# Row sums by TensorE in the expert part of a decoder kernel, and ScalarE's gelu of the dots moved within its beat

## The reference

```python
q = (xt @ wq).reshape(t, PEER_HEADS, 2, PEER_KEY_DIM)
sc = jnp.einsum('thcd,hcnd->thcn', q, keys)
# top 16 of each half, top 16 of their pair sums: 8 heads x 16 = 128 experts per token
gate = jax.nn.softmax(top, axis=-1)
act = jax.nn.gelu(jnp.einsum('td,tkd->tk', xb, u[ib]))      # u: 16384 x 1024
y = jnp.einsum('tk,tkd->td', gb * act, v[ib])               # v: 16384 x 1024
h = h + y
```

## Time and profile before

| | |
|---|---|
| median of 3 runs | 3909.01 us (3907.59 to 3911.07) |
| the profiled execution | 3902.45 us |
| its span | 3900.3 us |
| busy: PE, DVE, ACT, POOL | 3177.5, 2572.0, 813.4, 922.5 us |
| mean granted clock of TensorE | 0.886 of full |
| moved by DMA | 943.26 MB, mean 242 GB/s |

### The profile page before, as it was taken

How to read it: one execution, slowest core, us unless ns; L and a number is a source line. 1 busy time by engine, 2 the same in 40 slices (tenths; PEclk the granted TensorE clock), 3 DMA queues, 4 the chain that set the end, 5 groups by cost and what they waited for, 6 DMA issues and landing times. The chain is left out here.

```text
span 3900.3 us, 38895 instructions
## 1 busy us (share of the span) xinstructions
PE 3177.5 (81%) x12836; PEld 2259.9 (58%) x12836; DVE 2572.0 (66%) x5206; ACT 813.4 (21%) x1764; POOL 922.5 (24%) x888
## 2 busy tenths in 40 slices
PE   6947877876699999999578478777766999999995
PEld 5725566765466666565266256666755665665652
DVE  3574554899876666666746634548998766666666
ACT  2331323236300000000033313231463000000000
POOL 0011201237422222222200122022373222222221
PEclk9969878986799999999889788788867999999997
DMA  3100112269999999999731001121799999999997
GB/s 102 54 0 1 48 37 78 67 224 287 317 408 417 416 417 417 417 417 405 307 97 38 1 1 48 44 81 65 244 290 330 413 416 417 416 417 417 413 402 289
DMA packets 235338, 943.26 MB, mean 242 GB/s; under 512 B 19584, under 2 KB 85632, under 8 KB 164864
## 3 DMA queue, kind: packets, MB, share of 16 engines
q0 software_dynamic: 73728, 536.90, 34.8%
q1 hardware_dynamic: 95360, 370.31, 24.9%
q10 hardware_dynamic: 66048, 33.56, 2.9%
HBM read 904.52 MB, written 35.65 MB: 241 GB/s over the span
## 5 line engine op out<-in xcount | busy, mean ns | idle before, releaser
L1873 PE MATMUL bank<-peer_x_late,xT 128*128 128x256 f32 x4096 | 953.7, 388 | 128.9 <-DMA xT<-in_peer_ut 82.6
L1873 PEld LDWEIGHTS bank<-peer_x_late,xT 128*128 128x128 f32 x4096 | 790.5, 195 | 350.4 <-DMA xT<-in_peer_ut 124.6
L1980 DVE CUSTOM_DVE_ANT_0 peer_slots<-peer_slots,wide 128x1024 f32<-128x1024 f32 x512 | 626.7, 1224 | 539.0 <-DMA peer_slots<-in_peer_uv,peer_rows 537.7
L1823 POOL DMA_INDIRECT peer_slots<-in_peer_uv,peer_rows x512 | 515.0, 1006 | 1547.3 <-DVE h L1992 1433.7
L1884 PE MATMUL bank<-ring,peer_acts_u 128*128 128x512 f32 x1344 | 614.7, 602 | 59.6 <-issue 38.9
L1992 DVE SCALAR_TENSOR_TENSOR h<-peer_slots,peer_coef,h 128x1024 f32<-128x1024 f32 x512 | 657.0, 1283 | 9.3
L1884 PEld LDWEIGHTS bank<-ring,peer_acts_u 128*128 128x128 f32 x1344 | 255.1, 192 | 339.7 <-issue 304.9
L1914 ACT ACTIVATE peer_coef<-peer_dots 128x2 f32<-128x2 f32 x256 | 51.7, 202 | 1373.0 <-DVE peer_dots L1980 1373.0
L1884 PE MATMUL bank<-ring,wide 128*128 128x512 f32 x704 | 324.0, 605 | 12.3 <-DVE wide L2000 12.0
L1862 PE MATMUL bank<-peer_hot 128*128 128x128 f32 x1024 | 224.1, 389 | 96.6 <-POOL peer_hot L1832 56.3
L1862 PEld LDWEIGHTS bank<-peer_hot 128*128 128x128 f32 x1024 | 197.1, 286 | 124.1 <-ACT peer_hot L1927 82.5
(11 more groups left out here) (455 smaller groups left out, 4036.3 us busy)
## 6 DMA issues: line engine op xcount, KB each, us to landing
xT<-in_peer_ut SPq DMA_DIRECT2D x256, 512.0 KB, 21.4
ring<-in_peer_uv SPq DMA_DIRECT2D x256, 512.0 KB, 21.4
gates<-peer_staging ACTq DMA_DIRECT2D x32, 1024.0 KB, 7.1
peer_staging<-gates SPq DMA_DIRECT2D x32, 1024.0 KB, 24.4
ring<-in_w_in SPq DMA_DIRECT2D x48, 512.0 KB, 3.6
ring<-in_peer_wq SPq DMA_DIRECT2D x32, 512.0 KB, 3.6
nsa_w<-in_cmp_w SPq DMA_DIRECT2D x2, 4096.0 KB, 12.1
ring<-in_w_out SPq DMA_DIRECT2D x16, 512.0 KB, 4.5
```

The source lines that it names most:

```text
L1823: nc.gpsimd.indirect_dma_start(out=p.slots[:, n % ROW_SLOTS, :], out_offset=None, in_=A["peer_uv"], in_offset=bass.IndirectOffsetOnAxis(ap ...
L1873: last = nc.tensor.matmul(k.bank[bank_of[j]][:, 0:DENSE], u_raw[:, j % U_RING, b * P:(b + 1) * P], p.x_late[:, b, :], start=b == 0, stop=b ...
L1980: nc.vector.tensor_tensor_reduce(out=u, in0=u, in1=k.wide[:, t, :], scale=1.0, scalar=0.0, op0=ALU.mult, op1=ALU.add, accum_out=p.dots[:, ...
```

## The change

Steps 0 to 47 (`EARLY`, those until four beats before the gates are done; all are of chunk 0) are summed in another way. ScalarE takes the gelu of each dot alone (`gelu_early`). Two steps later VectorE multiplies it by its gate (`coef_early`) and GpSimd makes a diagonal matrix of the 128 coefficients (`diagonal`, a 128 x 128 operation, ring of four). Three steps later TensorE multiplies the v rows by the diagonal, two matmuls of 512 columns, and adds them up in banks 5 and 6 over all early steps (`add_row` on TensorE). In beat 80 VectorE adds the two banks to `h` (`take_early`); the first V tile, which uses the same banks, waits for that.

`steps_until` is changed: 8 steps by beat 24, then three in four beats until beat 78. GpSimd no longer does the fourth gating of a quad, ScalarE does all four. ScalarE's gelu of dots stands last in its beat. `RUN_AHEAD` is 18 for 20, and the buffers of activated U tiles 20 for 22.

```diff
@@ -1509,9 +1509,9 @@
 LAG = 4
 BATCH = 2
 TILES = P
-ACTS = 22
-OWN_ACTS = 14
-RUN_AHEAD = 20
+ACTS = 20
+OWN_ACTS = 12
+RUN_AHEAD = 18
 GELU_LAG = 2
 U_RING = 4
 V_RING = 4
@@ -1537,15 +1537,21 @@
     beat = max(beat, 0)
     chosen = CHOOSE_AT[3] + PIECES
     if beat <= chosen:
-        return beat // 4
-    first = chosen // 4
+        return beat // 3
+    first = chosen // 3
     if beat <= TILES_AT - 4:
-        return first + (beat - chosen) // 2
-    first += (TILES_AT - 4 - chosen) // 2
+        return first + (beat - chosen) * 3 // 4
+    first += (TILES_AT - 4 - chosen) * 3 // 4
     if beat <= TILES_AT:
         return first + beat - (TILES_AT - 4)
     first += 4
     return first + (min(beat, BEATS) - TILES_AT) * (STEPS - first) // TILES
+
+
+LAST_EARLY = TILES_AT - 5
+EARLY = steps_until(LAST_EARLY + 1)
+DIAGONALS = 4
+COEF_LAG, SUM_LAG = 2, 3
 
 
 def u_until(beat):
@@ -1756,8 +1762,8 @@
 
 
 
-    with stage(nc, "dve_done", "shifted", "exps", "indexed", "chosen", "turned", "kept", "hot1", "hot2", "hot1_act", "hot1_pool", "spread", "copied",
-               "stored0", "stored1", "u_done", "gelus_u", "gated", "v_done", "dots", "gelus", "coefs", "summed", "y_added",
+    with stage(nc, "dve_done", "shifted", "exps", "indexed", "chosen", "turned", "kept", "hot1", "hot2", "hot1_act", "spread", "copied",
+               "stored0", "stored1", "u_done", "gelus_u", "gated", "v_done", "dots", "gelus", "early_gelus", "early_coefs", "diagonals", "coefs", "summed", "early_in", "y_added",
                "g_in0", "g_in1", *[f"u_in{n}" for n in range(U_RING)], *[f"v_in{n}" for n in range(V_RING)]) as (block, s):
         row_in = k.row_in
         u_in = [s[f"u_in{n}"] for n in range(U_RING)]
@@ -1824,20 +1830,23 @@
                                              in_offset=bass.IndirectOffsetOnAxis(ap=p.rows[:, t, pick:pick + 1], axis=0),
                                              ).then_inc(row_in[n % ROW_SLOTS], 16)
 
-            def last_gate(q):
-                if q % (QUADS // 2) == 0:
-                    pool.wait_ge(s["kept"], q // (QUADS // 2) + 1)
-                pool.wait_ge(s["hot1"], q + 1)
-                hot = p.hot1[:, 4 * (q % 2) + 3, :]
-                nc.gpsimd.tensor_scalar(hot, hot, p.picks[:, 2, 4 * q + 3:4 * q + 4], None, ALU.mult).then_inc(s["hot1_pool"], 1)
+            def diagonal(m):
+                pool.wait_ge(s["early_coefs"], m + 1)
+                if m >= DIAGONALS:
+                    pool.wait_ge(s["summed"], m - DIAGONALS + 1)
+                nc.gpsimd.tensor_scalar(p.diagonal[:, m % DIAGONALS, :], k.ident[:, :], p.coef[:, 0, m:m + 1], None,
+                                        ALU.mult).then_inc(s["diagonals"], 1)
             for n in range(ROW_SLOTS):
                 gather(n)
             for beat in range(BEATS):
-                if 0 <= beat - QUADS_AT < QUADS:
-                    last_gate(beat - QUADS_AT)
                 for n in now(steps_until, beat):
+                    if COEF_LAG <= n < EARLY:
+                        diagonal(n - COEF_LAG)
                     if n >= LAG and n - LAG + ROW_SLOTS < STEPS:
                         gather(n - LAG + ROW_SLOTS)
+                if beat == LAST_EARLY:
+                    for m in range(EARLY - COEF_LAG, EARLY):
+                        diagonal(m)
             for n in range(ROW_SLOTS):
                 pool.wait_ge(row_in[n], 16 * len(range(n, STEPS, ROW_SLOTS)))
 
@@ -1853,7 +1862,6 @@
 
             def spread_quad(q):
                 pe.wait_ge(s["hot1_act"], q + 1)
-                pe.wait_ge(s["hot1_pool"], q + 1)
                 pe.wait_ge(s["hot2"], q + 1)
                 if q >= 2:
                     pe.wait_ge(s["copied"], q - 1)
@@ -1874,11 +1882,20 @@
                                             start=b == 0, stop=b == DB - 1)
                 last.then_inc(s["u_done"], 1)
 
+            def add_row(m):
+                pe.wait_ge(s["diagonals"], m + 1)
+                for half in range(2):
+                    last = nc.tensor.matmul(k.bank[5 + half][:, :], p.diagonal[:, m % DIAGONALS, :],
+                                            p.slots[:, m % ROW_SLOTS, DM + half * 512:DM + (half + 1) * 512],
+                                            start=m == 0, stop=m == EARLY - 1)
+                last.then_inc(s["summed"], 1)
+
             def with_v(j):
                 pe.wait_ge(v_in[j % V_RING], 16 * (j // V_RING + 1))
                 pe.wait_ge(s["gated"], j + 1)
                 if j == 0:
                     pe.wait_ge(s["kept"], 2)
+                    pe.wait_ge(s["early_in"], 2)
                 for t in range(2):
                     for half in range(2):
                         last = nc.tensor.matmul(k.bank[4 + 2 * t + half][:, :], act_of(j)[:, t * P:(t + 1) * P],
@@ -1890,6 +1907,12 @@
                         turn(t)
                 if 0 <= beat - QUADS_AT < QUADS:
                     spread_quad(beat - QUADS_AT)
+                for n in now(steps_until, beat):
+                    if SUM_LAG <= n < EARLY:
+                        add_row(n - SUM_LAG)
+                if beat == LAST_EARLY:
+                    for m in range(EARLY - SUM_LAG, EARLY):
+                        add_row(m)
                 for j in now(u_until, beat):
                     with_u(j)
                 if beat >= TILES_AT:
@@ -1913,6 +1936,10 @@
                 act.wait_ge(s["dots"], (g + 1) * BATCH)
                 nc.scalar.activation(p.coef[:, t, at:at + BATCH], p.dots[:, t, at:at + BATCH], ACT.Gelu_apprx_tanh).then_inc(s["gelus"], 1)
 
+            def gelu_early(n):
+                act.wait_ge(s["dots"], n + 1)
+                nc.scalar.activation(p.coef[:, 0, n:n + 1], p.dots[:, 0, n:n + 1], ACT.Gelu_apprx_tanh).then_inc(s["early_gelus"], 1)
+
             def gelu_u(j):
                 act.wait_ge(s["u_done"], j + 1)
                 if j >= ACTS:
@@ -1922,7 +1949,7 @@
             def gates(q):
 
                 act.wait_ge(s["hot1"], q + 1)
-                for n in range(3):
+                for n in range(4):
                     hot = p.hot1[:, 4 * (q % 2) + n, :]
                     last = nc.scalar.activation(hot, hot, ACT.Copy, scale=p.picks[:, 2, 4 * q + n:4 * q + n + 1])
                 last.then_inc(s["hot1_act"], 1)
@@ -1948,15 +1975,17 @@
                         keep(t)
                 if beat == EXPS_AT[1]:
                     exps(1)
-                for n in now(steps_until, beat):
-                    if n % BATCH == BATCH - 1:
-                        gelu_step(n // BATCH)
                 if 0 <= beat - QUADS_AT < QUADS:
                     gates(beat - QUADS_AT)
                 if 0 <= beat - 1 - QUADS_AT < QUADS:
                     copy_quad(beat - 1 - QUADS_AT)
                 for j in now(u_until, beat - GELU_LAG):
                     gelu_u(j)
+                for n in now(steps_until, beat):
+                    if n < EARLY:
+                        gelu_early(n)
+                    elif n % BATCH == BATCH - 1:
+                        gelu_step(n // BATCH)
 
         @block.vector
         def _(dve):
@@ -1984,13 +2013,24 @@
                 t, pick = m // PICKS, m % PICKS
                 if m % BATCH == 0:
                     c = slice(pick, pick + BATCH)
-                    dve.wait_ge(s["gelus"], m // BATCH + 1)
+                    dve.wait_ge(s["gelus"], (m - EARLY) // BATCH + 1)
                     nc.vector.tensor_tensor(p.coef[:, t, c], p.coef[:, t, c], p.gate[:, t, c], ALU.mult).then_inc(s["coefs"], 1)
-                    dve.wait_ge(s["coefs"], m // BATCH + 1)
-                if m:
-                    dve.wait_ge(s["summed"], m)
+                    dve.wait_ge(s["coefs"], (m - EARLY) // BATCH + 1)
+                dve.wait_ge(s["summed"], m)
                 nc.vector.scalar_tensor_tensor(out=k.h[:, t, :], in0=p.slots[:, m % ROW_SLOTS, DM:2 * DM], scalar=p.coef[:, t, pick:pick + 1],
                                                in1=k.h[:, t, :], op0=ALU.mult, op1=ALU.add).then_inc(s["summed"], 1)
+
+            def coef_early(m):
+                dve.wait_ge(s["early_gelus"], m + 1)
+                nc.vector.tensor_tensor(p.coef[:, 0, m:m + 1], p.coef[:, 0, m:m + 1], p.gate[:, 0, m:m + 1],
+                                        ALU.mult).then_inc(s["early_coefs"], 1)
+
+            def take_early():
+                dve.wait_ge(s["summed"], EARLY)
+                for half in range(2):
+                    o = slice(half * 512, (half + 1) * 512)
+                    nc.vector.tensor_tensor(k.h[:, 0, o], k.h[:, 0, o], k.bank[5 + half][:, :], ALU.add).then_inc(s["early_in"], 1)
+                dve.wait_ge(s["early_in"], 2)
 
             def gate_tile(j):
                 dve.wait_ge(s["gelus_u"], j + 1)
@@ -2008,9 +2048,16 @@
                 if 0 <= beat - QUADS_AT < QUADS:
                     hots(beat - QUADS_AT)
                 for n in now(steps_until, beat):
+                    if COEF_LAG <= n < EARLY:
```

(9 more changed lines are left out.)

## The result

The changed kernel takes 3891.67 us (median of 7 runs, 3874.32 to 3897.88) against 3911.07 us (7 runs, 3906.94 to 3919.35) for the kernel before, run beside it: a ratio of 0.9946, 95% interval 0.9933 to 0.9958. It is 19 us faster where the forecast was 42 us; 3891.67 lies inside the stated range of 3838 to 3905, but 25 us above the 3867 forecast and just outside the 3845 to 3890 that the forecast called its likeliest case.

What follows compares the result with a forecast made beforehand. DMA was taken to bound the tile stretch, TensorE close behind; the gate stretch had nothing full. Per layer +1 + 8 - 30 = -21, two layers -42, from 3902.45 to 3860.5, plus 6.6 for the runs' median: 3867 us, range 3838 to 3905.

Steps and rivals of the forecast that it cites:

- before beat 24 +1: Beats before 24: two U tiles go, five TensorE sums come; +1 us a layer, bounds 0 and +3.
- gate stretch +8: Beats 24 to 77: 39 gathers and 13 stores make DMA need 151 us against 143.1; bounds +1 and +29.
- gap nothing: Between gate and tile stretch: taking in two banks costs some 1.4 us while VectorE is otherwise free, so no change.
- tile stretch and tail −30: 15 gathers fewer, two U tiles more: -35.7 us by bytes, 5 to 6 kept for DMA-TensorE waits; bounds -20 and -36.
- It is cover only: ScalarE has 19 us left: Gate stretch: ScalarE's work sums to 132 us; moving the gelu last removes a wait DMA was not expected to feel.
- the late diagonal's rival: Gate stretch: GpSimd's diagonal-and-gather chain sets the step, some 4.0 us each, 156 us; 3877 us, up to 3895; 7%.
- the 144 to 156 us: Sign expected in the profile after: gate stretch of 144 to 156 us; over 165 us the prediction is wrong.
- The price of a gather: Gate stretch: 2.71 us of DMA time per 1.049 MB gather, taken from the mixed stretch; alternatives 2.53 and 3.24.
- the rival with cheap gathers: Cheap gathers, full DMA: gate stretch +1, tile part -35.7, early +1; -34 us a layer, 3841 us; 17%.
- The rival at 1.2 GHz: TensorE stays at half clock in the gate stretch: 218 us there, +46 a layer, 4001 us; 6%.
- The rival of the port: Gate stretch: each diagonal holds the shared port and delays a dot by 0.62 us; VectorE 151 us, 3873 us; 3%.
- the rival that tile beats don't shorten: Tile stretch: TensorE's waits are not for bytes, so beats stay 7.32 us; +5 a layer, 3919 us; 5%.

Runs made afterwards that it cites:

- the version with late gelus: Changed kernel with a third staging part for gate stores and the gelus of the first four dots three beats later: 3851.28 us, ratio 0.9857.
- SyncE: Changed kernel with third staging part and first four dots' gelus three beats later, gate stores issued by SyncE instead of ScalarE: 3846.48 us, ratio 0.9842.
- the third part: Changed kernel with a third staging part for gate stores, so a copy waits for the store three before it, not two: 3855.02 us, ratio 0.9863.
- the control: Kernel before with the third staging part alone: 3906.82 us beside 3909.46, ratio 0.9994.
- the old pace: Changed kernel with the step schedule of the kernel before, early sums still by TensorE, two staging parts: 3920.73 us, ratio 1.0032.
- gelu first: Gelus of dots ahead of gatings and copies again: changed kernel 3890.78 us, ratio 0.9955; with third staging part 3887.02 us, ratio 0.9948.
- the pace alone: Kernel before with only the new step schedule, row additions still by VectorE: 3898.99 us, ratio 0.9969.
- The late gelus: Changed kernel with the gelus of the first four dots three beats later in ScalarE's order, nothing else: 3880.54 us, ratio 0.993.
- gating on GpSimd: Changed kernel with third staging part and first four dots' gelus three beats later, fourth gating of each quad back on GpSimd: 3882.25 us, ratio 0.9926.
- sums at the old pace with the third part: Changed kernel with the step schedule of the kernel before and a third staging part for gate stores: 3898.0 us, ratio 0.9974.

## Why the prediction came out as it did, step by step

**The sum.** Forecast a layer: before beat 24 +1, gate stretch +8, gap nothing, tile stretch and tail −30: −21. Measured on the same cuts (hot pair of beat 24, hot pair of beat 77, first V tile; two layers before, four after): +4.6, +16.7 (159.9 for 143.2), +4.5, −34.5 (19.0 and 15.5): −8.7. The table, which cuts at copies, has the same sum as +7.7, +14.8, +3.5 and −34.5. The sign and the large term were right; the three small terms cost 17 us a layer more than forecast, and the large one gave 4.5 of them back. That the time fell inside the range is partly luck: gathers priced too dear and a tile part priced too cautiously made up for a part of the waits that were left out.

**Gate stretch: the step that failed** is the sentence on ScalarE, "It is cover only: ScalarE has 19 us left", together with pricing the stretch as the DMA engines' work alone. ScalarE's busy time was right (forecast 132 us at most, measured 115), but its queue holds the copy that waits for a store, and a store has a landing time besides its share of the engines. Both numbers were in the trace of before: the part is wanted again 13.1 us after the store's issue, and the store landed after 7.1 us. That is 6 us of slack, in a stretch whose queues I was about to fill. It landed after 16.0 in the median, and up to 23.1. I had it only in passing, in the late diagonal's rival ("with the gelu or store waits behind it"), without a price. With three parts a store has nine beats, mostly 22 to 25 us: medians of 17.7 and 18.3 us (the version with late gelus) are not awaited, one of 22.0 (SyncE) is in part. Shown by the third part (−19.4 us of stretch from copy to copy), the control (0) and the old pace. Of the signs that the prediction gave, the gate stretch missed the 144 to 156 us (159.2 and 162.7) but stayed under the 165 that was named as refuting it.

**The price of a gather** was over-estimated, and by luck this hid half of the miss: without the store's waits the stretch takes 142.3 and 143.2 us, 8 less than the 151 forecast, and the waits put 17 on top. I took 2.71 us. In the changed kernel's stretch it is 65.0% of 159.18 us for 38.2 gathers (40.05 MB), 2.71 again; with the third part 70.7% of 138.66 for 37.9, 2.59. The store is 3.62 and 3.58 us. So the rival with cheap gathers (144 us) was right on its own mechanism once the store is out of the way: DMA share 1.03, and 3855 us where it gave 3841. But a gather has no fixed price here that a stretch could be added up from. At the old pace it stays at 2.98 us with a share of 1.02, at the new pace it is 2.90 with VectorE's additions and 2.75 with the gelu first, at a share of 1.01. The Trainium skill (DMA: Bandwidth & Descriptors, Queues, rings and completion order) has the engines serve their queues in turn, a packet at a time. The traces agree in so far as a gather costs least where no gate stores stand beside it, 2.53 us in the tile stretch; they don't show single turns. By the same rule a store in small packets (13.50 MB in 26560, some 508 bytes each, if these are the packets that the page means) that takes turns with gathers (40.05 MB in 5497) should land later the more gathers stand beside it; the rise from 7.1 to 16.0 us agrees, but no run here changed the packets' size alone.

**VectorE, GpSimd and TensorE** went as worked out. VectorE was busy 116 us (forecast 127), GpSimd 97 (98 to 126), with the diagonals at 1274 ns in the mean; TensorE 129 us at a clock of 0.92 (forecast 117 at full clock). The clock went with TensorE's work: 0.60 before, with TensorE busy 70% of the stretch, 0.56 with the pace alone (60%), 0.98 with sums and no stall (89%). The rival at 1.2 GHz did not come. The rival of the port: dots took 1225 ns with diagonals beside them, 1215 before, and GpSimd's operations are the ones stretched. Where the Trainium skill (SBUF — State Buffer, SBUF: two separate sides) has whichever starts second blocked, the traces show hardly anything but GpSimd's slowed. In the trace of before, 60 dots begin inside a gating, and the longest took 1.22 us; in that of after, 21 begin inside a diagonal, at 1244 ns in the mean and 1.36 us at most. (The profile calls GpSimd's spans rough.) That rival and the late diagonal (TensorE has no wait for a diagonal in the gate stretch) are out.

**The gelu last** was forecast to matter only as cover. As the change stands nothing can be told of it (gelu first: the same time); once the store wait is gone it is worth 32 us. It is needed for the shorter stretch, and the store wait kept the changed kernel from it.

**Before beat 24: +4.6 for +1.** I counted durations on TensorE and VectorE, not ScalarE's order. All of it is in the choose stage; from the first hot pair to that of beat 24 both kernels take 39.0 us. (The 3.1 us that the table has under first quads lie behind that hot pair: the copy of quad 10 follows it after 7.4 us, before after 4.5.) The pace alone costs 3.3 us before beat 24. The late gelus bring the changed kernel from +4.6 to +1.7: the gelu of an early dot stood ahead of U tiles' gelus and of the copy of the picks, for which the first hot pair waits.

**Gap: +4.5 for nothing** (+3.5 in the table's cut). In that cut it varies between 18.8 and 29.8 us over four layers of the changed kernel, and with the stretch before it. The pace alone has +3.3 there without any sums, and the sums at the old pace have none, so it seems to come with the pace; what in the pace makes it stays open.

**Tile stretch and tail: −34.5 for −30**, between the forecast and the −35.7 of pure bytes. TensorE's waits for U tiles in the first layer's tile stretch fell from 26.5 us to:

```profile
PE bank L1881 <- DMA xT<-in_peer_ut: 7.0, 3, 2.7
```

The 5 to 6 us kept back for the coupling of DMA and TensorE were too many by 4.5. A beat with a U tile takes 767.56/109 = 7.04 us for 7.32; the rival that tile beats don't shorten is refuted.

## What to carry to other kernels

A buffer that a store must leave before it is written again is a clock of its own: write down, for each such ring, how many us of work lie between issue and reuse and how long the store takes to land now, and ask what the change does to both. The share of the queues doesn't say when a transfer lands, and since the same gather took 2.59 to 3.24 us of it here, not what the next one will cost either. Two waits on one engine can stand in for each other, so a part of a change that is worth nothing when undone alone can be worth the most once another wait is gone: undo parts in pairs as well as one by one.

## What the runs showed of the hardware that was not expected

- A 1 MB gate store took 3.5 to 3.8 us of the DMA engines' time in the gate stretches of all runs in which the stores have a queue to themselves, but landed after 7.1 us in the median with the queues at 91% and 286 GB/s (kernel before), 12.7 at 95% and 322 GB/s (pace alone), 16.0 at 95% and 337 GB/s (changed), 14.6 at 99% and 345 GB/s (gating on GpSimd) and 17.7 to 18.3 at 103% and 381 GB/s (third part, late gelus). It rises with what the queues move, if not strictly. In the changed kernel long landings and landings of 5.4 to 6.0 us follow each other.
- The issue of such a store can hold the issuing engine itself: 0.52 us as a rule, up to 6.36 us on ScalarE (third part) and 11.37 us on SyncE. What it waits for the trace doesn't say, and fullness is not all of it: 6.01 us at a share of 0.97 (sums at the old pace with the third part), none over 0.6 us at 0.99 (gating on GpSimd).
- The DMA time of the same gather was 3.24 us before, 2.90 with the pace alone, 2.71 in the changed kernel and 2.59 with the third part, but 2.98 at the old pace with a share of 1.02. A share of 1 was read at 138.7 and at 151.9 us for the same work.
- A GpSimd 128 x 128 multiplication took 0.62 us alone in the trace of after and 1.75 us in the mean where it began inside one of VectorE's dots. The gatings took 1301 ns in the mean before, and 1049 and 1136 ns where VectorE has no row additions; that version differs in GpSimd's order too. VectorE's dots took 1214 to 1244 ns in the mean in the gate stretches of all runs.
